# Two-block transformer step: keys and values of the memory in two normalisations per layer, two modulation rows per layer on VectorE

## What is computed

```python
h = layer_norm(ALPHA * h + 0.5 * swiglu(h, ffn1...), ...)
z = h @ w_in[l]
...
mix = jnp.concatenate([y_conv, y_rec, y_pool], axis=-1) @ w_out[l]
h = layer_norm(ALPHA * h + mix, ...)
h = layer_norm(ALPHA * h + cross_attn(h, mem, ca_q[l], ca_k[l], ca_v[l], ca_o[l]), ...)
h = layer_norm(ALPHA * h + 0.5 * swiglu(h, ffn2...), ...)
```

## Time and profile before

| | us |
|---|---|
| median of three runs | 3507.94 (3505.67 to 3511.57) |
| the profiled execution | 3485.94 |
| its span (first to last instruction) | 3484.1 |
| TensorE busy | 3186.7 |
| VectorE busy | 2093.4 |
| GpSimd busy | 1175.5 |
| ScalarE busy | 936.2 |
| TensorE's granted clock, mean | 0.988 of full speed |

### The profile page before, as it was taken

How to read it: one execution, slowest core, us unless ns; L and a number is a source line. 1 busy time by engine, 2 the same in 40 slices (tenths; PEclk the granted TensorE clock), 3 DMA queues, 4 the chain that set the end, 5 groups by cost and what they waited for, 6 DMA issues and landing times.

```text
span 3484.1 us, 46503 instructions
## 1 busy us (share of the span) xinstructions
PE 3186.7 (91%) x16293; PEld 2515.7 (72%) x16293; DVE 2093.4 (60%) x4171; ACT 936.2 (27%) x2393; POOL 1175.5 (34%) x1129
## 2 busy tenths in 40 slices
PE   8899999999999999999999898878888888978887
PEld 5698878778878878778867655438877855626777
DVE  6686778555555448555544585576554477477544
ACT  2310022120010022111023354334443354433333
POOL 1003643234425423244410143343431033344332
PEclk9999999999999999999999999999999999999999
DMA  8578987689979977688953899999995399999998
GB/s 343 187 264 325 391 343 258 251 336 344 352 279 384 351 262 260 247 332 342 354 196 116 311 393 418 419 421 407 420 421 237 122 393 414 419 421 420 421 421 360
DMA packets 246943, 1163.11 MB, mean 334 GB/s; under 512 B 27256, under 2 KB 29656, under 8 KB 180720
## 3 DMA queue, kind: packets, MB, share of 16 engines
q0 software_dynamic: 152784, 825.30, 59.0%
q1 hardware_dynamic: 93936, 335.48, 26.5%
q10 hardware_dynamic: 48, 0.05, 0.0%
HBM read 1159.62 MB, written 1.10 MB: 333 GB/s over the span
## 4 chain that ended last, share of the span: by engine, by line
PE 60%; DMA 22%; DVE 6%; ACT 5%; issue 3%; POOL 1%; SPq 0%; ACTq 0%; DVEq 0%; POOLq 0%
DMA ring<-in_peer_uv,idx 20%; PE ps_b L1035 17%; PE ps_a L1043 8%; PE ps_b L589 8%; PE ps_a L970 5%; PE ps_a L576 5%; PE ps_b L840 3%; PE ps_a L974 3%; ACT arena L1204 3%; PE ps_b L598 2%; DVE arena L1998 1%; DMA ring<-in_ffn 1%; ACT L1204 1%; PE ps_b L640 1%; ACT wts L1204 1%
## 5 line engine op out<-in xcount | busy, mean ns | idle before, releaser
L1998 DVE SCALAR_TENSOR_TENSOR arena<-ring,h_tm 128x1024 f32<-128x1024 f32 x512 | 625.3, 1223 | 519.4 <-DMA ring<-in_peer_uv,idx 518.6
L553 POOL DMA_INDIRECT ring<-in_peer_uv,idx x512 | 538.9, 1053 | 1157.3 <-PE ps_a L970 431.6
L515 POOL DMA_INDIRECT ring<-in_peer_uv,idx_now x512 | 566.3, 1106 | 415.8 <-DVE arena L1916 163.0
L1035 PE MATMUL ps_b<-x_t,ring 128*128 128x256 f32 x2816 | 622.1, 379 | 5.1 <-ACT x_t L1204 2.7
L974 PE MATMUL ps_a<-arena,ring 128*128 128x128 f32 x4096 | 520.5, 284 | 108.4 <-ACT arena L1204 107.8
L1035 PEld LDWEIGHTS ps_b<-x_t,ring 128*128 128x128 f32 x2816 | 534.4, 190 | 80.4 <-DMA ring<-in_ffn 4.5
L974 PEld LDWEIGHTS ps_a<-arena,ring 128*128 128x128 f32 x4096 | 483.8, 195 | 146.1 <-ACT arena L1204 145.3
L970 PE MATMUL ps_a<-ring,arena 128*128 128x512 f32 x1024 | 486.2, 610 | 85.0 <-ACT arena L1204 84.5
L1204 ACT ACTIVATE arena<-ps_b 128x256 f32<-128x256 f32 (+2 forms) x219 | 107.5, 493 | 1330.1 <-PE ps_b L1035 830.0
L970 PEld LDWEIGHTS ps_a<-ring,arena 128*128 128x128 f32 x1024 | 182.5, 192 | 334.0 <-ACT arena L1204 177.2
L1043 PE MATMUL ps_a<-arena,ring 128*128 128x256 f32 x1408 | 317.6, 379 | 0.0
(11 more groups left out here) (262 smaller groups left out, 3189.8 us busy)
## 6 DMA issues: line engine op xcount, KB each, us to landing
ring<-in_ffn SPq DMA_DIRECT2D x264, 512.0 KB, 7.4
wring<-in_second_w SPq DMA_DIRECT2D x232, 512.0 KB, 4.5
wring<-in_mix_w SPq DMA_DIRECT2D x128, 512.0 KB, 5.6
ring<-in_ada_rows POOLq DMA_DIRECT2D x36, 512.0 KB, 7.0
ring<-in_peer_uv,idx_now POOLq DMA_INDIRECT x512, 8.6
ring<-in_peer_uv,idx POOLq DMA_INDIRECT x512, 12.7
ring<-in_second_w SPq DMA_DIRECT2D x4, 512.0 KB, 15.8
ring<-in_c_rows POOLq DMA_DIRECT2D x1, 1024.0 KB, 7.4
```

The costliest lines, as they stand in the source:

```text
L515: G.indirect_dma_start(rows[:, s, :], None, table, bass.IndirectOffsetOnAxis(ap=idx_now[:, half, s:s + 1], axis=0)).then_inc(rows_in[s], p ...
L553: G.indirect_dma_start(pairs[:, slot, :, :].rearrange("p c d -> p (c d)"), None, a["peer_uv"], bass.IndirectOffsetOnAxis(ap=idx[:, b, s:s ...
L1035: ins = mm(bank[:, part * T:(part + 1) * T], fw[:, ft % 2, part, k * P:(k + 1) * P], x_t[:, k, :], start=k == 0, stop=k == KT - 1)
L1998: V.scalar_tensor_tensor(products[n % 2], pairs[:, at % PAIRS, 0, :], 1.0, h_tm[:, n // SLOTS, :], ALU.mult, ALU.mult, accum_out=dots[:, n ...
```

## The change

1. The first value group (group 12) moves into each layer's first normalisation, and the last key group (group 19) into its second, in place of the modulation row there: 4 products ahead of the mean, 7 ahead of the variance, 5 behind it (`value_between`, `key_between`). Six groups of keys and values are left in the mixer. The pooling product moves ahead of the last of them. The value group has a place of its own (`ca_v0`). The chunks of `mix_w` are laid out in the new order.
2. The third and fourth normalisation keep their row on TensorE.
3. The two rows that this leaves over per layer are made by VectorE (`mod_row_sums`): 8 steps over 512 columns, each a partition-wise product with silu(c) added to the sum so far, ahead of the last hidden tile of each feed forward; TensorE then sums over the partitions with one product of two columns (times D in ScalarE's copy, as the constant matrix holds 1/D), ahead of the last down projection. It is done for c alone: both stored rows are the same, and `ROW_AT` gives these places rows whose `c_ctx` part is not used. VectorE releases all four slots of `wring` at its end.
4. SyncE loads the row for the fourth normalisation behind the second feed forward's weights, no longer ahead of them.
5. In layer 0's first feed forward four expert dots fewer stand before the sums (`SEARCH_DOTS` 3 in place of 7), so four more behind the normalisation. Clearing the edges (three memsets) moves from ahead of that normalisation to behind it.

```diff
-SEARCH_DOTS = (0, 0, 2, 2, 2, 2, 4, 4, 4, 4, 4, 4, 6, 5, 5, 5, 5, 5, 5, 6, 7, 3)
+SEARCH_DOTS = (0, 0, 2, 2, 2, 2, 4, 4, 4, 4, 4, 4, 6, 5, 5, 5, 5, 5, 5, 6, 3, 3)
+ROW_AT = 0, 1, 4, 2, 5, 3, 6, 7, 8, 9, 10, 11
...
                     else:
                         chunk_loads(a["mix_w"], mix_at + (MIX_CHUNKS - WR), WR)
+                        mod_row_loads(row_at + 1)
                         mod_row_loads(row_at + 2)
-                        mod_row_loads(row_at + 3)
...
                     if w == 0:
-                        chunk_loads(a["mix_w"], mix_at, 48)
-                        mod_row_loads(row_at + 1)
-                        chunk_loads(a["mix_w"], mix_at + 48, MIX_CHUNKS - WR - 48)
+                        chunk_loads(a["mix_w"], mix_at, MIX_CHUNKS - WR)
+                    else:
+                        mod_row_loads(row_at + 3)
...
                 gate_up(FT - 1)
                 down(FT - 2)
+                eng.wait_ge(chunk_done, pe.now(chunk_done))
+                mm(ps_d[0:2, :], mean_d[:, 0:2], row_acc, start=True, stop=True).then_inc(
+                    row_summed, pe.adds(row_summed))
                 down(FT - 1, True)
...
-            def layer_norm():
-                mod_row_part(1, 0, 1)
+            def layer_norm(between):
+                between(0, 4)
                 mean_of_pairs(ps_c[:, 0:T], resid_pairs).then_inc(mean_done, pe.adds(mean_done))
-                mod_row_part(1, 1, 2)
+                between(4, 8 if between == mod_row_between else 11)
+                if between != mod_row_between:
+                    mod_row_free()
                 mean_of_pairs(ps_d[:, 0:T], square_pairs).then_inc(var_done, pe.adds(var_done))
-                mod_row_part(1, 2, WR)
+                between(8 if between == mod_row_between else 11, 16)
...
+            def value_between(i0, i1):
+                for i in range(i0, i1):
+                    b, k = i // KT, i % KT
+                    if b == 0 and k % 4 == 0:
+                        chunk(k // 4)
+                    ins = mm(ps_b[:, b * T:(b + 1) * T], mem_t[:, k, b * P:(b + 1) * P],
+                             wring[:, k // 4, (k % 4) * T:(k % 4 + 1) * T], start=k == 0, stop=k == KT - 1)
...
-                for g in range(15, 20):
-                    group(g, 2 * g, mem_t, tm=g < 16)
-
+                for g in range(16, 18):
+                    group(g, 2 * g, mem_t)
                 eng.wait_ge(pooled_sums, pe.next(pooled_sums))
                 for t in range(2):
                     at = fc["pool_w"][0] + t * P
                     ins = mm(ps_d[:, t * T:(t + 1) * T], cur[:, at:at + P], pool_p[:, t, :], start=True, stop=True)
                 ins.then_inc(pool_mm_done, pe.adds(pool_mm_done))
+                group(18, 36, mem_t)
...
+            def mod_row_sums(l, w):
+                loads = ROW_LOADS + l * (MIX_CHUNKS // WR + 4) + w * (MIX_CHUNKS // WR + 2)
+                for k in range(KT):
+                    part, weight = wring[:, k // 2, k % 2 * 512:(k % 2 + 1) * 512], cond[:, 2 * k:2 * k + 1]
+                    if k % 2 == 0:
+                        eng.wait_ge(weights_in[k // 2], 16 * loads)
+                    if k == 0:
+                        ins = V.tensor_scalar(row_acc, part, weight, None, ALU.mult)
+                    else:
+                        eng.wait_ge(row_step, ve.now(row_step))
+                        ins = V.scalar_tensor_tensor(row_acc, part, weight, row_acc, ALU.mult, ALU.add)
+                    if k < KT - 1:
+                        ins.then_inc(row_step, ve.adds(row_step))
+                ins.then_inc(chunk_done, ve.adds(chunk_done, WR))
...
                     turn_end(summing, i, at + HEAD_SLOTS)
+                mod_row_sums(l, w)
                 hidden_tile(FT - 1)
```

More of the change, by code:

```diff
@@ L1083, in _ @@
                 feed_forward(h_have)
-                layer_norm()
+                layer_norm(value_between)
                 def group(g, c, src, ready=None, tm=False):
[L1087 to L1091, removed]
+                    eng.wait_ge(z_done, pe.now(z_done, 1))
+                    odd = (g + 1 if g < 12 else g) % 2
+                    bank = ps_b[:, odd * 512:(odd + 1) * 512]
                     if tm:
@@ L1112, in _ @@
                 for g in range(4):
-                    group(g, 2 * g, x_t, h_take if g == 0 else None)
+                    group(g, 2 * g + 2, x_t, h_take if g == 0 else None)
                 for g in range(4, 12):
-                    group(g, 2 * g, x_t, tm=g < 6)
+                    group(g, 2 * g + 2, x_t, tm=g < 6)
                     level(g - 4)
-                group(12, 24, mem_t, tm=True)
+                group(13, 26, mem_t, tm=True)
                 level(8)
-                group(13, 26, mem_t, tm=True)
+                group(14, 28, mem_t, tm=True)
                 eng.wait_ge(level_taken, pe.next(level_taken, 2))
@@ L1128, in _ @@
                 ins.then_inc(o_done, pe.adds(o_done))
-                group(14, 28, mem_t, tm=True)
+                group(15, 30, mem_t, tm=True)
                 for j in range(2):
@@ L1232, in mod_row_take @@
             def mod_row_take(i, bank, row):
-                eng.wait_ge(chunk_done, ac.next(chunk_done, WR))
+                if bank == 2:
+                    eng.wait_ge(row_summed, ac.next(row_summed))
+                    ac.skip(chunk_done, WR)
+                else:
+                    eng.wait_ge(chunk_done, ac.next(chunk_done, WR))
                 if i >= 2:
@@ L1238, in mod_row_take @@
                     eng.wait_ge(mod_row_out[1 - i % 2], ac.now(mod_row_out[1 - i % 2]))
-                act(row[0:2, :], ps_b[0:2, bank * 512:(bank + 1) * 512], ACT.Copy).then_inc(
-                    mod_row_taken, ac.adds(mod_row_taken))
+                ps, scale = (ps_d[0:2, :], float(D)) if bank == 2 else (ps_b[0:2, bank * 512:(bank + 1) * 512], 1.0)
+                act(row[0:2, :], ps, ACT.Copy, scale=scale).then_inc(mod_row_taken, ac.adds(mod_row_taken))
                 eng.wait_ge(mod_row_taken, ac.now(mod_row_taken))
-                nc.scalar.dma_start(mod_rows[:, i * 512:(i + 1) * 512], row[0:2, :]).then_inc(
+                at = ROW_AT[i] * 512
+                nc.scalar.dma_start(mod_rows[:, at:at + 512], row[0:2, :]).then_inc(
                     mod_row_out[i % 2], ac.adds(mod_row_out[i % 2], 16))
@@ L1553, in _ @@
                 feed_forward()
+                mod_row_take(row_at, 2, mod_row)
                 layer_norm(0)
-                mod_row_take(row_at, 1, mod_row)
+                eng.wait_ge(chunk_done, ac.next(chunk_done, 2))
+                act(ca_v0, ps_b[:, 0:512].rearrange("p (b t) -> p b t", t=T), ACT.Copy).then_inc(
+                    z_done, ac.adds(z_done))
                 if l == 0:
@@ L1585, in _ @@
                 exps(8)
-                for g in range(12, 14):
+                for g in range(13, 15):
                     group(g, ca_v[:, g - 12])
@@ L1596, in _ @@
                                           bias=eps[:, 1:2]).then_inc(o_std_done, ac.adds(o_std_done))
-                group(15, ca_v[:, 3])
-                for g in range(16, 20):
+                for g in range(16, 18):
                     group(g, ca_k[:, 2 * g - 32:2 * g - 30, :])
@@ L1603, in _ @@
                 ins.then_inc(pooled_done, ac.adds(pooled_done))
+                group(18, ca_k[:, 4:6, :])
                 peer_gelu()
@@ L1606, in _ @@
                 layer_norm(1)
-                mod_row_take(row_at + 1, 1, mod_row)
+                group(19, ca_k[:, 6:8, :])
                 for g in range(20, 24):
@@ L2186, in searching_feed_forward, with clear_edges @@
                     at += SEARCH_DOTS[q]
+                    if q == FT - 2:
+                        mod_row_sums(0, 0)
+                eng.wait_ge(row_used, ve.now(row_used))
+            def clear_edges():
                 eng.wait_ge(dve_step, ve.now(dve_step))
@@ L2192, in searching_feed_forward, with feed_forward @@
                 V.memset(pool_u[:, :, 0:16], 0.0).then_inc(dve_step, ve.adds(dve_step))
-                eng.wait_ge(row_used, ve.now(row_used))
-            def feed_forward(h, summing):
+            def feed_forward(l, w, h, summing):
                 at = SLOTS - FF_SLOTS if summing else 0
@@ L2270, in _ @@
                     eng.wait_ge(dve_step, ve.now(dve_step))
-                eng.wait_ge(z_done, ve.next(z_done, 2))
+                eng.wait_ge(z_done, ve.next(z_done, 3))
                 eng.wait_ge(layer_vecs, ve.now(layer_vecs))
```

78 lines of the change are left out of this document (54 added, 24 removed).

## The result

The changed kernel took 3482.2 us (median of 4 executions, 3478.1 to 3486.5) beside 3506.8 us for the kernel before (3502.9 to 3511.6): ratio 0.9926, 95% interval 0.9914 to 0.9938. That is 24.6 us less; forecast were 25.4 less and 3482.5 us.

A forecast was written before the change was run, and what follows sets the result against it. TensorE, busy for 91% of the span, was taken to bound the kernel. The terms, -27.6 + 3.6 - 1.9 - 0.3 + 0.5 + 0.3 = -25.4 us, took the median of 3507.94 to 3482.5 us, range 3476 to 3489.

The forecast's parts named there:

- Groups out of the mixer, -27.6 and -1.9: Mixer: two groups fewer per layer on TensorE, 27.6 us gone; a group behind the pooling product hides a wait, 1.9 us.
- Normalisations unchanged: Changed normalisations: VectorE and ScalarE set their length, so the groups placed there add 0 us.
- first rival: TensorE's clock falls after 1.7 us idle in the four changed normalisations: 7 us, so 3489.5; chance 0.07.
- the rule named beside it: Trainium skill: pauses between matmuls that grow too long send TensorE to its low clock; said to favour the clock's fall.
- The row's product, +3.6: Ahead of each feed forward's last down projection: one narrow 512-column product on TensorE, 0.90 us, four times, 3.6 us back.
- The sums, 0: Feed forward ends: VectorE's row sums, 5.9 us each, are covered before the last hidden tile is wanted; cost 0.
- Loads for the filler: Start of the normalisations: weight loads into wring, released late by VectorE, come slightly late; 0.3 us in all.
- the third rival: Normalisations: filler starves on slow weight loads, 36 us lost against 25.4 gained, so 3519 us; chance 0.05.
- Layer 0's gates, +0.5 within 0 to 1.5: Behind layer 0's first normalisation: clearing and 16 dots delay the forget gates' scaling, which ScalarE's logarithm awaits; 0.5 us taken.
- one of the signs of being wrong: Layer 0's first level: TensorE waiting over 2 us for the edge or gate work would show the prediction wrong.
- The sum: Whole kernel: all terms together, -25.4 us; 26.2 less at the good end, about 20.3 at the bad end.
- The 22 us between profile and median: Whole kernel: the median of runs, 3507.94 us, lay 22 us above the profiled execution, 3485.94; carried into the forecast.

The follow-up runs named there:

- e7: The changed kernel with the product of the pooling behind the last of the mixer's groups again, as in the kernel before; one execution took 3488.2 us.
- e1: The kernel before with modulation rows cut to two-column products in the two normalisations around the mixer: 3499.2 us, ratio 1.0030 to the kernel before.
- e3: The changed kernel with 16 steps in place of 8 in each of VectorE's row sums: 3509.2 us, ratio 1.0004 to the kernel before.
- e4: The changed kernel with layer 0's edge clearing and 4 of 16 expert dots behind the scaling of the forget gates: 3478.6 us, ratio 0.9917 to the kernel before.
- e6: The changed kernel with edges and 4 dots behind the gates' scaling, plus three unused products in each cross attention: 3471.4 us, ratio 0.9881 to the kernel before.

## Why the prediction was right, and where it was off

- **Groups out of the mixer, -27.6 and -1.9: right.** Layer 1 from its first group to the projection takes 149.0 to 149.1 us in the four profiles of the changed kernel, and 163.9 to 164.2 in three of the kernel before: 15.0 for 13.8 + 0.93. e7 shows the 0.93.
- **Normalisations unchanged: right**, 10.7 us before and after at a clock of 1.00. e1 adds what the prediction had only as its first rival: left empty they lose the clock, and the kernel is 11 us longer. That rival (the clock falls at a pause of 1.7 us) did not come; the pause is 1.65 us and harmless. Nor did the rule named beside it speak for it: that is one for pauses that grow too long, and this one had not.
- **The row's product, +3.6: right.** The four feed forwards take 929.8 us in the mean of three profiles before and 933.6 in that of the four after. **The sums, 0: right**, though a step takes 0.80 to 0.82 us, not 0.73, and the slack is 1.5 us where 2.4 were worked out: the prediction asked when the down projection wants the hidden tile, but the sum's own product stands ahead of it and wants the sum 0.95 us sooner. e3 shows the cliff behind it.
- **Loads for the filler: right.** No normalisation of the changed kernel begins with a wait for wring; the third rival, which stood on it, fell.
- **Layer 0's gates, +0.5 within 0 to 1.5: the step that failed.** The term counted eight gathers at 1.25 to 1.8 us and a landing 7.9 us behind the issue. In the trace the eighth is issued 13.0 us behind the first (1.86 each), its dot starts 9.7 us behind that, and each of the last seven dots waits for its own gather, 8.1 us in all where the kernel before waited 3.2. TensorE waits 2.0, 2.8, 2.5 and 3.6 us for the level where it waited for nothing, and in the last three of these the level then runs at the lower clock, +1.0 to 1.5. A wait of over 2 us there is one of the signs of being wrong that the prediction named. Layer 0 gained 11.0 us in the mean where layer 1 gained 15.0: the term is about 4 us. e4 and e6 show that the cause is the order on VectorE, since the wait goes with it.
- **The sum.** -15.0 - 11.0 + 4.0, and 0.5 less ahead of the means, make -22.5. The four measurements gave 24.6, 18.9, 27.2 and 21.4 us less, in the mean 23.0. The first, by which 25.4 looks all but exact, is 1.6 us on the good side of that: the mechanism and the large terms were right, one small term was 3.5 us too good, and the scatter hid it. That 3482.2 us lies within 0.3 of the forecast is luck. The 22 us between profile and median the prediction carried over without a reason; that came right because both kernels have the stall.

## What to carry to other kernels

A stretch whose length other engines set is free room on the bound engine, and work that stood on its stream elsewhere can be moved into it one to one; but on TensorE the room is also what keeps its clock, so fill it with products of full width, and count a wait as long as those of e3 (3.2 to 4.9 us) at 1.4 times its length. When VectorE takes over work, look for the narrow place in its order (here a logarithm behind 16 dots), not at its busy share. And before a profile and a median are compared, take both on the same chip.

## What the runs showed of the hardware

- In the first block of all 14 profiles TensorE went on at 2.4 GHz behind every pause of up to 2.13 us. Behind every pause of 2.84 us and more that found it at 2.4 GHz, some of the products ran at 1.2. In between it differed by execution: the same wait of 2.75 us, at the start of layer 1's first feed forward, was followed by a fall in 6 of the 14. In the cross attention a pause of 2.9 us filled with products whose results are thrown away left the clock at 1.00.
- On the chips of one kind TensorE stood still for 6 to 9 us at one place of the program in both layers, in both kernels and in every variant, with no cause in the profile; on the one chip of the other kind it never did. It was not found out what it is. With the slower products behind it, it is some 18 us of the kernel, nearly as much as the change gave.
